# The rotary exchange of rows in the first block, by a permutation matmul on TensorE or by a shuffle on VectorE from the projection's PSUM bank

## The reference, cut to what matters

```python
def rotate(x, cos, sin):
    x1, x2 = jnp.split(x, 2, axis=-1)
    return jnp.concatenate([x1 * cos - x2 * sin, x2 * cos + x1 * sin], axis=-1)
...
    q = jnp.concatenate([rotate(q[..., :ROPE_DIM], cos, sin), q[..., ROPE_DIM:]], axis=-1)
    k = jnp.concatenate([rotate(k[..., :ROPE_DIM], cos, sin), k[..., ROPE_DIM:]], axis=-1)
...
    q = rotate(q, cos, sin)
    k = rotate(k, cos, sin) * (R_QK_DIM ** -0.5)
```

## Time and profile before

| what | value |
|---|---|
| median of 3 runs | 3921.5 us (3919.44 to 3929.78) |
| the profiled execution, its own time | 3918.32 us |
| its span on the core | 3916.4 us |
| PE busy | 3709.7 us, 95% |
| DVE busy | 1857.9 us, 47% |
| ACT busy | 1110.0 us, 28% |
| POOL busy | 1421.8 us, 36% |
| granted PE clock, mean | 0.981 of 2.4 GHz |

### The profile page before, as it was taken

How to read it: one execution, slowest core, us unless ns; L and a number is a source line. 1 busy time by engine, 2 the same in 40 slices (tenths; PEclk the granted TensorE clock), 3 DMA queues, 4 the chain that set the end, 5 groups by cost and what they waited for, 6 DMA issues and landing times.

```text
span 3916.4 us, 43068 instructions
## 1 busy us (share of the span) xinstructions
PE 3709.7 (95%) x16664; PEld 2834.0 (72%) x16664; DVE 1857.9 (47%) x2125; ACT 1110.0 (28%) x1817; POOL 1421.8 (36%) x734
## 2 busy tenths in 40 slices
PE   6989999999999999999999998899899989999998
PEld 5666788887877666788887876777666668766666
DVE  3665113223157555113223148962666589345654
ACT  3334100112212334210112212123465321335542
POOL 1212344432356222344342356433322345333324
PEclk9999999999999999999999998999899989999999
DMA  4000111111133100111111123211111231111122
GB/s 148 28 27 27 51 51 46 44 51 33 36 121 108 33 27 27 46 51 46 48 46 34 40 81 94 93 43 33 33 32 31 94 98 49 33 33 33 32 71 86
DMA packets 75580, 209.40 MB, mean 53 GB/s; under 512 B 9120, under 2 KB 14496, under 8 KB 74912
## 3 DMA queue, kind: packets, MB, share of 16 engines
q1 hardware_dynamic: 52992, 156.98, 13.8%
q10 hardware_dynamic: 22432, 50.18, 3.4%
HBM read 186.16 MB, written 20.97 MB: 53 GB/s over the span
## 4 chain that ended last, share of the span: by engine, by line
PE 85%; DVE 9%; ACT 4%; issue 1%; ACTq 1%; DMA 0%; DVEq 0%
PE psA L502 45%; PE psT L483 16%; PE psA L483 5%; PE psA L1820 3%; PE psA L731 2%; PE psT L1885 2%; PE psT L781 2%; PE psT L1791 1%; PE psT L1796 1%; DVE b_rowmax L1274 1%; DVE Hlo L2311 1%; PE psT L1864 1%; ACT X L994 1%; PE psT L1861 1%; PE psT L703 1%
## 5 line engine op out<-in xcount | busy, mean ns | idle before, releaser
L449 POOL TENSOR_TENSOR Whi<-stage,credit 128x1024 fp32r<-128x1024 f32 (+2 forms) x364 | 605.5, 1664 | 2446.9 <-PE psA L502 1213.2
L452 POOL TENSOR_TENSOR Wlo<-stage,Whi 128x1024 fp32r<-128x1024 f32 (+2 forms) x364 | 815.9, 2242 | 28.5
L502 PE MATMUL psA<-Hhi,Whi 128*128 128x512 f32 x2240 | 703.7, 395 | 11.9 <-ACT b_wk L2054 11.9
L502 PE MATMUL psA<-Hlo,Whi 128*128 128x512 f32 x2240 | 691.1, 390 | 0.0
L502 PE MATMUL psA<-Hhi,Wlo 128*128 128x512 f32 x2240 | 690.8, 390 | 0.0
L502 PEld LDWEIGHTS psA<-Hhi,Whi 128*128 128x128 f32 x2240 | 420.1, 188 | 113.0 <-issue 28.1
L502 PEld LDWEIGHTS psA<-Hlo,Whi 128*128 128x128 f32 x2240 | 421.1, 188 | 88.4
L502 PEld LDWEIGHTS psA<-Hhi,Wlo 128*128 128x128 f32 x2240 | 421.1, 188 | 88.2
L483 PE MATMUL psT<-Hhi,Whi 128*128 128x512 f32 x1024 | 424.8, 415 | 35.0 <-ACT b_upad L1017 18.8
L483 PE MATMUL psT<-Hhi,Wlo 128*128 128x512 f32 x1024 | 404.4, 395 | 0.0
L483 PE MATMUL psT<-Hlo,Whi 128*128 128x512 f32 x1024 | 404.1, 395 | 0.0
(11 more groups left out here) (301 smaller groups left out, 4996.9 us busy)
## 6 DMA issues: line engine op xcount, KB each, us to landing
stage<-in_w SPq DMA_DIRECT2D x232, 512.0 KB, 3.5
stage<-in_w SPq DMA_DIRECT2D x68, 256.0 KB, 2.6
xs<-X ACTq DMA_DIRECT2D x64, 256.0 KB, 3.2
stage<-in_w SPq DMA_DIRECT2D x32, 384.0 KB, 3.1
b_wk<-xs ACTq DMA_DIRECT2D x36, 256.0 KB, 4.9
b_wk<-in_x ACTq DMA_DIRECT2D x8, 512.0 KB, 11.3
rope<-in_ropes ACTq DMA_DIRECT2D x4, 1024.0 KB, 7.2
stage<-in_w SPq DMA_DIRECT2D x32, 128.0 KB, 2.1
```

The lines of the kernel that those rows point to most:

```text
L449: pool.tensor_tensor(Whi[:, b, 0:n], stage[:, b, 0:n], credit[:, 0:1].broadcast_to([P, n]), ALU.add).then_inc(s.w_hi, 1)
L452: pool.tensor_tensor(Wlo[:, b, 0:n], stage[:, b, 0:n], Whi[:, b, 0:n].bitcast(F32), ALU.subtract).then_inc(s.w_split, 1)
L502: mm = pe.matmul(dst[h], w[:, cols], r[k][:, h * HALF:(h + 1) * HALF], start=first and k == order[0] and r is rhi and w is whi, stop=last ...
```

## The change

Rotation no longer uses PE. DVE reads the projection's PSUM bank itself: a stream shuffle writes the exchanged rows to SBUF, a product of the bank with the cosine table writes the destination and frees the bank, and a product with the sine table and a sum follow. ACT's copies of q and k are gone, as are both permutation matrices and their two loads at the start. The shuffle permutes inside groups of 32 partitions, so in the retention, where 32 are exchanged with 32, the weight columns and the tables are reordered on the host (`PAIRED`) and the exchange is 16 with 16. `B1_PRELUDE` and `B1_SLOTS` lose the sq and sk pieces, and DVE does its rotation as its part of the q and k pieces, so in their place.

```diff
-B1_PRELUDE = [("q", 0, 0), ("k", 0, 0), ("sq", 0, 0), ("sk", 0, 0), ("q", 0, 1), ("k", 0, 1), ("sq", 0, 1),
-              ("sk", 0, 1), ("v", 0, 0), ("v", 0, 1)]
+B1_PRELUDE = [("q", 0, 0), ("k", 0, 0), ("q", 0, 1), ("k", 0, 1), ("v", 0, 0), ("v", 0, 1)]
 B1_SLOTS = [([("vt", 0, 0)], [("q", 1, 0), ("x0", 0, 0, True)]),
             ([("vt", 0, 1)], [("q", 1, 1), ("x0", 0, 1, True)]),
-            ([("sq", 1, 0)], [("k", 1, 0), ("b0", 0, 0, True), ("ss", -1, 1)]),
-            ([], [("sq", 1, 1), ("k", 1, 1), ("b0", 0, 1, True)]),
-            ([("sk", 1, 0)], [("z", 0, 0)]),
-            ([("sk", 1, 1)], [("z", 0, 1)]),
+            ([], [("k", 1, 0), ("b0", 0, 0, True), ("ss", -1, 1)]),
+            ([], [("k", 1, 1), ("b0", 0, 1, True)]),
+            ([], [("z", 0, 0)]),
+            ([], [("z", 0, 1)]),
             ([("v", 1, 0), ("x1", 0, 0, True)], [("ss", 0, 0), ("x1", 0, 1, True)]),
...
+def exchange(half):
+
+    return [i ^ half if i < 2 * half else i for i in range(32)]
...
-            for k, dst in ((K.swapa, swapa), (K.swapr, swapr)):
-                act.dma_start(dst[:], env.consts[:, k:k + P]).then_inc(swaps_in, 16)
...
-                swap(L, ("swaprq", 0), ("rq", 0), swapr, R_RAWQ)
-                swap(L, ("swaprk", 0), ("rk", 0), swapr, R_RAWK)
...
-                if kind in ("q", "k", "v"):
+                if kind == "v":
                     act.wait_ge(*F.filled(L, use))
-                    dst = {"q": AQ[h % 2], "k": AK[h % 2], "v": RAW}[kind]
-                    act.activation(dst[:, c], psF, ACT.Copy).then_inc(F.freed(use), 1)
+                    act.activation(RAW[:, c], psF, ACT.Copy).then_inc(F.freed(use), 1)
...
+            def rotate(L, use, dst, done):
+
+                raw = psA[:, A.buf(use)]
+                dve.wait_ge(*A.filled(L, use))
+                if use[0] == "rk":
+                    dve.wait_ge(*r_rot.upto(L, 2 * use[1] + 1))
+                step(dve.stream_shuffle(R_ROT, raw, exchange(16)))
+                dve.tensor_tensor(dst, raw, rope[:, 0], ALU.mult).then_inc(A.freed(use), 1)
+                step(dve.tensor_tensor(R_ROT, R_ROT, rope[:, 1], ALU.mult))
+                dve.wait_ge(*A.drained(L, use))
                 dve.tensor_tensor(dst, dst, R_ROT, ALU.add).then_inc(done, 1)
...
-                if kind in ("sq", "sk"):
-                    dst = (AQ if kind == "sq" else AK)[h % 2][:, c]
+                if kind in ("q", "k"):
+                    dst = (AQ if kind == "q" else AK)[h % 2][:, c]
                     dve.wait_ge(*F.filled(L, use))
-                    dve.tensor_tensor(ROT, psF, rope[:, 1, c], ALU.mult).then_inc(F.freed(use), 1)
-                    step(dve.tensor_tensor(dst, dst, rope[:, 0, c], ALU.mult))
+                    step(dve.stream_shuffle(ROT, psF, exchange(8)))
+                    dve.tensor_tensor(dst, psF, rope[:, 0, c], ALU.mult).then_inc(F.freed(use), 1)
+                    step(dve.tensor_tensor(ROT, ROT, rope[:, 1, c], ALU.mult))
                     dve.wait_ge(*F.drained(L, use))
                     dve.tensor_tensor(dst, dst, ROT, ALU.add).then_inc(rotated.sem, 1)
```

More of the change, by code:

```diff
@@ L355 @@
     mask = 256
[L356 to L364, removed]
+    swapm = 384
+    causal = 512
+    dmask = 640
+    xi = 640 + 512
+    zeta = 640 + 768
+    decay = 640 + 1024
+    n = 640 + 1024 + 2
 def build(nc, x, w1, par1, lamv, finalg, w2, par2, pww, sgw, sgb, consts, ropes, ng, out, xs):
@@ L579, in first_block @@
         summed, rstd, h_scaled, h_hi, h_lo = env.summed, env.rstd, env.h_scaled, env.h_hi, env.h_lo
-        consts_in, params_in, swaps_in, rtab_in = (sem(n) for n in ("consts_in", "params_in", "swaps_in", "rtab_in"))
+        consts_in, params_in, rtab_in = (sem(n) for n in ("consts_in", "params_in", "rtab_in"))
         x_in = [sem(f"x_in{t}") for t in range(NT)]
@@ L619, in first_block @@
         SUM, SUM2 = psT[:, 1, HALF:], psT[:, 1, 0:HALF]
[L621 to L622 removed]
+        Q, KK, V = wk[:, 0], wk[:, 1], wk[:, 2]
+        RSQ, R_ROT, R_RAWV = upad[:, 2:], rraw[:, 0], rraw[:, 1]
         KZ, SM, KS, ST, QX = wk[:, 4], wk[:, 4], wk[:, 5], wk[:, 6], wk[:, 7]
@@ L710, in turn @@
                 return mm
[L712 to L716, removed]
             def scores(L, h, q):
@@ L751, in piece @@
                     pe.wait_ge(s.w_split, L * NP + p + 3)
-                if kind in ("sq", "sk", "vt"):
-                    source = ({"sq": "q", "sk": "k", "vt": "v"}[kind], h, half)
+                if kind == "vt":
+                    source = ("v", h, half)
                     if F.buf(source) != F.buf(use):
@@ L763, in piece @@
                                          arrived if kind == "q" and h == 0 else None)
-                elif kind in ("sq", "sk"):
-                    mm = pe.matmul(psF, swapa[:], (AQ if kind == "sq" else AK)[h % 2][:, c], start=True, stop=True)
                 elif kind == "vt":
@@ L786, in attention @@
                 for use in B1_PRELUDE:
-                    if L == 0 and use == ("sq", 0, 0):
+                    if L == 0 and use == ("q", 0, 1):
                         turn_tokens(1)
-                        pe.wait_ge(swaps_in, 32)
                     piece(L, use)
@@ L926, in tensor @@
                 chunk_outputs(L, 1)
-                swap(L, ("swaprq", 1), ("rq", 1), swapr, R_RAWQ)
                 head_squares(L, 1)
@@ L930, in tensor @@
                 panel(L, ("rv", 2), Hhi, Hlo)
-                swap(L, ("swaprk", 1), ("rk", 1), swapr, R_RAWK)
                 panel(L, ("rz", 2), Hhi, Hlo)
@@ L1290, in piece @@
                 c, psF = slice(half * HALF, (half + 1) * HALF), bank(use)
-                if kind in ("sq", "sk"):
-                    dst = (AQ if kind == "sq" else AK)[h % 2][:, c]
+                if kind in ("q", "k"):
+                    dst = (AQ if kind == "q" else AK)[h % 2][:, c]
                     dve.wait_ge(*F.filled(L, use))
-                    dve.tensor_tensor(ROT, psF, rope[:, 1, c], ALU.mult).then_inc(F.freed(use), 1)
-                    step(dve.tensor_tensor(dst, dst, rope[:, 0, c], ALU.mult))
+                    step(dve.stream_shuffle(ROT, psF, exchange(8)))
+                    dve.tensor_tensor(dst, psF, rope[:, 0, c], ALU.mult).then_inc(F.freed(use), 1)
+                    step(dve.tensor_tensor(ROT, ROT, rope[:, 1, c], ALU.mult))
                     dve.wait_ge(*F.drained(L, use))
                     dve.tensor_tensor(dst, dst, ROT, ALU.add).then_inc(rotated.sem, 1)
-                    dve.wait_ge(*rotated.upto(L, rotations(h, kind[1], half)))
+                    dve.wait_ge(*rotated.upto(L, rotations(h, kind, half)))
                 elif kind == "vt":
@@ L1571, in vector @@
                 dve.wait_ge(*rope_in.upto(L, 32))
-                rotate(L, ("swaprq", 0), ("rq", 0), R_RAWQ, Q, r_rot.sem)
-                rotate(L, ("swaprk", 0), ("rk", 0), R_RAWK, KK, r_rot.sem)
+                rotate(L, ("rq", 0), Q, r_rot.sem)
+                rotate(L, ("rk", 0), KK, r_rot.sem)
                 dve.wait_ge(rtab_in, 16)
@@ L1582, in vector @@
                 states(L, 1)
-                rotate(L, ("swaprq", 1), ("rq", 1), R_RAWQ, Q, r_rot.sem)
+                rotate(L, ("rq", 1), Q, r_rot.sem)
                 head_tail(L, 1)
-                rotate(L, ("swaprk", 1), ("rk", 1), R_RAWK, KK, r_rot.sem)
+                rotate(L, ("rk", 1), KK, r_rot.sem)
                 decayed(L, 1)
@@ L2593, in _panel @@
     return w.reshape(nk, P, m).transpose(1, 0, 2).reshape(P, nk * m)
+PAIRED = np.r_[0:16, 32:48, 16:32, 48:64]
 def _pack1(w_in, w_branch, w_out):
@@ L2607, in _pack1 @@
             w = w_in[:, c:c + P]
+            if name[0] in ("rq", "rk"):
+                w = w[:, np.r_[PAIRED, A_QK + PAIRED]]
         out.append(_panel(w, nk))
@@ L2644, in _tables @@
     t[:, K.mask:K.mask + P] = np.where(idx[None, :] <= idx[:, None], 0.0, NEG)
[L2645 to L2649, removed]
     for r in range(M_ROPE):
@@ L2671, in _tables @@
         for m in range(P):
-            r = (m - base) % size
+            r = PAIRED[m % size] if n == 1 else (m - base) % size
             if m >= base and r < 2 * half:
```

11 lines of the change are left out of this document (2 added, 9 removed).

## The result

| | before | after |
|---|---|---|
| median on one chip | 3923.18 us (13 runs, 3912.01 to 3930.22) | 3936.24 us (13 runs, 3927.32 to 3938.80) |
| ratio, 95% interval | | 1.0031 [1.0021, 1.0041] |
| span of the profiled execution | 3916.4 us | 3925.5 us |
| mean granted PE clock in it | 0.981 | 0.975 |

The change costs 0.31%, 12 to 13 us. The interval doesn't contain 1, but the difference is hardly more than the 12 us that the prediction called the least that can be told. The forecast had given slower 0.47 and same 0.46. The profiled execution of the changed kernel is its fastest of 13, 9 us under its median, and that of the kernel before is 5 us under its own, so the two traces differ by 9.1 us where the medians differ by 13.1. The forecast was 3930 us, 3916 to 3946.

The account below looks back on a forecast made before the run. PE, holding the last chain for 85% of the span, was taken as the bound. Terms: -21.8 - 21.4 - 11.6 - 3.5 - 1.0 - 1.1 + 56.9 = -3.5, plus 15.2 clock: +11.7 on 3918.3 gives 3930 us, range 3916 to 3946.

Parts of the forecast that it names:

- The place and the waits: Attention slots 1 to 4: DVE's rotation stands ahead of the mix that PE's transpositions need; new PE waits, +56.9 us.
- The shuffle: DVE's added instruction per rotation: 0.68 us for 512 columns, taken from a PSUM copy, 0.72 with its wait.
- second rival: A shuffle takes 1.4 us instead of 0.68, 15 us in all, so 3945; chance 0.18, shared with falls at nearly every wait.
- (a): Attention slots: 24 permutation matmuls of 0.91 us leave PE, 21.8 us gained.
- (b): Attention: PE's bank waits of 1.57 us (second z panel) and 2.99 us (second k panel) go, 9.4 and 12.0 us.
- (c): Retention: eight swaps of 1024 columns leave PE, six at 1.74 us and two at 0.6, 11.6 us gained.
- (d): Preludes: four swaps of 512 columns each, 0.87 us apiece; 3.5 us gained in layer 1, 1.0 kept in layer 0.
- (e): Start: ACT issues two loads fewer, 0.55 us each, so its first work begins 1.1 us earlier.
- the prelude of layer 0: Swaps gone, but k's second panel waits some 2.8 us for the first q bank; 1.0 of 3.5 us gain kept.
- The clock: PE's granted clock falls at 8 in 14 of 19 waits: 10.9 falls of 1.4 us, +15.2 us.
- the likeliest case: The forecast with 6 to 16 falls of PE's clock, +5 to +19 us; chance 0.58.
- first rival: The waits are there but the clock holds in all but a few: -3.5 to +4 us, 3915 to 3922; chance 0.17.

Follow-up runs that it names:

- E3: The changed kernel with DVE making the next slot's mix before the rotation of a q or k piece: 3891.3 us, ratio 0.9924 to the kernel before.
- E4: The changed kernel with the attention's shuffle done twice in every rotation: 3961.91 us, ratio 1.011 to the kernel before.
- E6: The kernel before with the change in the retention alone, its attention as before: 3913.99 us, ratio 0.9977.
- E7: E3 with DVE's work on the last head's second value product also put behind mix(4): 3910.08 us, ratio 0.9973 to the kernel before.
- E1: The changed kernel with PE making the q and k pieces ahead of their slot's transpositions: 3893.8 us, ratio 0.9923 to the kernel before.

## Why the prediction was right

The forecast was 3930 us; 3936.2 was measured, and the profiled execution took 3927.3. Of the 6.3 us between, 4.9 lie in the trace that the forecast started from, which was that much below the median of 13 runs. The change itself was forecast at +11.7 us and measured at +13.1. Its steps, one by one:

**The place and the waits** (+56.9): right. Slot 1: 2.65 predicted, 2.54 measured; slot 2: 3.08 and 2.97; slot 3: 2.11 (heads 1 and 2) and 3.06 (head 0) predicted, 2.09 and 2.95 measured; slot 4: 1.55 and 0.9 predicted, 1.33 and 0.73 measured. Together 54.1 us. E3 shows that the place makes them: with DVE's order changed alone the ratio goes from 1.0031 to 0.9924.

**The shuffle** (0.68): 0.728 us, with a mask load of 14 ns ahead of it that adds nothing to be seen. The second rival falls; E4 gives 0.77 for one more.

**What is removed in the attention** ((a) and (b), -43.2): with the waits, +13.7 was forecast for both layers. The attentions lost 31.1 us, of which the ten falls took 16.2, and an eleventh at the first scores of layer 1 some 1.4 (from the first scores to slot 1 it is 14.7 us there, 13.3 in layer 0). That leaves +13.5. As the waits were 2.8 us shorter in all than forecast, the removal gave some 40.6 us instead of 43.2; where the difference lies stays open.

**Retention and prelude of layer 1** ((c), (d)): between the attentions I had 5.8 for four swaps and 3.5 for the prelude, 9.3; the table has 8.9. Behind attention 1 it has 7.6 where I had 5.8. These 1.8 us stay open; the code behind that retention is the same in both kernels.

**Start** ((e) and the prelude of layer 0): -2.1 forecast, -2.1 measured, and this is luck. The measured value holds a fall of the clock, 1.5 us, that the forecast counted elsewhere, so -3.6 stands against -2.1, and both parts of it were off. First ACT work, after:

```profile
15.49 1.28 ACT L1149 ACT_TABLE_LOAD   x1 [15.49 <-issue]
```

It begins 2.44 us earlier, not 1.1. The wait of k's second panel was 3.11 us where I had 2.8, so the prelude gave some 0.3 less than the 1.0 that I kept.

**The clock** (+15.2): the likeliest case, and right in its number of falls and nearly in their price. There were 11 falls in the attentions, ten of them at the 18 new waits, and one behind the wait in the prelude (10.9 forecast for these 19), and none there before. I had 1.4 us for a fall. Heads 1 and 2 run the same program, and head 1 kept the clock at the waits of slots 1 to 3 where head 2 lost it at all three. The transpositions of slot 4 of head 1, then of slots 1 and 4 of head 2, after:

```profile
224.51 0.33 PE L706 MATMUL psT<-ident,X 128*128 128x128 f32 x1 [1.34 <-DVE X L1267]
275.01 0.33 PE L706 MATMUL psT<-ident,X 128*128 128x128 f32 x1 [2.54 <-DVE X L1267]
311.64 0.33 PE L706 MATMUL psT<-ident,X 128*128 128x128 f32 x1 [1.33 <-DVE X L1267]
```

From slot 1 to slot 4 head 1 takes 224.51 - 192.49 = 32.02 us, head 2 takes 36.63: 1.54 us for each fall. Between the two whole traces the clock's share was smaller by up to 6.8 us, because the part behind attention 1 spent less time at 1.2 GHz than before. Nothing in the forecast had that; it is the difference of two executions, and the medians, 13.1 us apart, are the better measure.

Two premises were weak. The four waits of 2.99 us that kept the clock were one execution's luck, as E6 shows, and so the first rival's best argument was none. And the falls are not a matter of length alone: head 2 lost the clock at its waits of 2.54, 2.97 and 2.09 us, in both layers, and head 1 kept it in both at the same three. What decides it no run here shows.

## What to carry to other kernels

Work that an engine takes over stands somewhere in its program. If its first instruction waits for the end of another engine's long piece, everything behind it waits too: look at what stands there, and at how long that has been ready. Here the same instructions, one place later, were worth 1.1%. Before such a move, name who needs the buffer that the moved work frees: E3 paid 0.8 us for it, E7 4.9. And price a wait of PE of 2 to 3 us at its length plus a part of the clock, here 0.9 us on the mean (16.2 us for 18 waits), and don't take one execution's clock for the kernel's.

## What the runs showed of the hardware

- A product of VectorE that reads and writes SBUF alone, 128x384, took 0.48 us, and 2.23 us beside a split on POOL (E1). The rotation's sum (line 1280), with two inputs in SBUF, took 0.69 in the median and up to 2.78. Shuffles from PSUM stayed within 725 to 743 ns in 32. The Trainium skill ("SBUF — State Buffer", section "SBUF: two separate sides") says that VectorE and GpSimd share a pair of ports under an exclusive lock, which an operation with two SBUF inputs or in a two-port mode takes. The rows agree. In E1 the product ends at 194.25, 0.2 us behind the split. It has a single input, and its time grows about half as fast with the columns as that of mix's last instruction, which has two (0.35 us for 128 columns in both, 0.48 and 0.62 for 384), which fits a two-port mode.
- A shuffle of 1024 columns from PSUM took 1.32 us, of 512 0.73; a copy of 512 took 0.68.
- The clock fell in one execution and not in another at the same waits: of four waits of 2.99 us at none in the trace before, at all in E6. One fall took 1.5 to 1.6 us.
